# Two transformer blocks on one core in split float16: four norms by logarithm, joint probabilities in differential attention, and four edits at the stage borders

## The reference, cut to what matters

```python
# first block
h = h + mixer_block(rms_norm(h, g), ...)  # differential attention (4 heads, two softmaxes) and windowed GQA
h = h + swiglu(rms_norm(h, g), ...)
attn = softmax(s1) - lam * softmax(s2)    # differential attention, then einsum('bhqk,bkhe->bqhe', attn, v)
# second block, two layers: convolution and MLA; then NSA (compressed, selected and window keys)
x = x + rms_norm_2(m, norm_mix_post); x = x + rms_norm_2(sq_relu_mlp(h, w1, w2), norm_mlp_post)
y = xf * lax.rsqrt(jnp.mean(xf * xf, axis=-1, keepdims=True) + EPS)   # every rms_norm
blk = z[:, idx] + pe[:, None, :]          # NSA: compress(), pe is the bias row
```

## Time and profile before

| | |
|---|---|
| median of 3 runs | 2088.15 us (2085.74 to 2088.97) |
| the profiled execution's own time | 2086.16 us |
| its span in the trace | 2084.4 us |
| PE busy | 2008.0 us, 96% |
| DVE busy | 1183.9 us, 57% |
| ACT busy | 819.6 us, 39% |
| POOL busy | 33.5 us, 2% |
| mean granted TensorE clock | 0.992 of full speed |

### The profile page before, as it was taken

How to read it: one execution, slowest core, us unless ns; L and a number is a source line. 1 busy time by engine, 2 the same in 40 slices (tenths; PEclk the granted TensorE clock), 3 DMA queues, 4 the chain that set the end, 5 groups by cost and what they waited for, 6 DMA issues and landing times. The chain is left out here.

```text
span 2084.4 us, 27136 instructions
## 1 busy us (share of the span) xinstructions
PE 2008.0 (96%) x10509; PEld 945.3 (45%) x10514; DVE 1183.9 (57%) x2158; ACT 819.6 (39%) x1487; POOL 33.5 (2%) x35
## 2 busy tenths in 40 slices
PE   9989999999999999999999999997999999999997
PEld 4444444444444444444444444444544444444443
DVE  5976744546554337776576632358766646864222
ACT  4446733323333232346333322236377743432220
POOL 2000000000000002000000000000000000000000
PEclk9999999999999999999999999999999999999998
DMA  7300223324333322312233333308100031533311
GB/s 216 101 1 1 72 86 106 101 62 141 101 101 111 91 91 78 114 51 72 71 108 113 103 103 99 107 25 255 42 1 1 22 101 41 148 104 105 108 41 41
DMA packets 53191, 179.16 MB, mean 86 GB/s; under 512 B 6096, under 2 KB 9808, under 8 KB 52816
## 3 DMA queue, kind: packets, MB, share of 16 engines
q1 hardware_dynamic: 53072, 177.51, 28.1%
HBM read 174.34 MB, written 2.10 MB: 85 GB/s over the span
## 5 line engine op out<-in xcount | busy, mean ns | idle before, releaser
L1744 DVE SCALAR_TENSOR_TENSOR w_lo<-w_raw,w_hi 128x1024 f16<-128x1024 f32 x317 | 385.5, 1220 | 166.5 <-ACT w_hi L1389 155.6
L1389 ACT ACTIVATE w_hi<-w_raw 128x1024 f16<-128x1024 f32 x317 | 330.8, 1048 | 264.3 <-PE pS L944 258.7
L942 PE MATMUL pS<-xx,w_hi 128*128 128x512 f16 x928 | 351.7, 379 | 2.3 <-DVE xx L1759 1.4
L944 PE MATMUL pS<-xx,w_lo 128*128 128x512 f16 x928 | 351.7, 379 | 0.0
L943 PE MATMUL pS<-xx,w_hi 128*128 128x512 f16 x928 | 351.6, 379 | 0.0
L942 PE MATMUL pS<-arena,w_hi 128*128 128x512 f16 x918 | 347.9, 379 | 2.1 <-DVE arena L1759 1.5
L943 PE MATMUL pS<-arena,w_hi 128*128 128x512 f16 x918 | 347.9, 379 | 0.0
L944 PE MATMUL pS<-arena,w_lo 128*128 128x512 f16 x918 | 347.9, 379 | 0.0
L1398 ACT ACTIVATE arena<-src 128x512 f16<-128x512 f32 x106 | 68.5, 647 | 323.2 <-DVE src L2391 164.0
L1805 DVE TENSOR_TENSOR tmp<-pS,rs 128x512 f32<-128x512 f32 x98 | 67.5, 689 | 137.9 <-PE pS L944 137.9
L942 PEld LDWEIGHTS pS<-arena,w_hi 128*128 128x128 f16 x918 | 89.9, 98 | 111.9 <-DVE arena L1759 1.9
(11 more groups left out here) (331 smaller groups left out, 2643.2 us busy)
## 6 DMA issues: line engine op xcount, KB each, us to landing
w_raw<-in_w SPq DMA_DIRECT2D x317, 512.0 KB, 3.6
X<-in_x SPq DMA_DIRECT2D x8, 264.0 KB, 7.4
arena<-in_c SPq DMA_DIRECT2D x2, 1024.0 KB, 7.6
out_t<-X SPq DMA_DIRECT2D x8, 256.0 KB, 2.0
arena<-in_h SPq DMA_DIRECT2D x4, 256.0 KB, 13.1
arena<-in_h SPq DMA_DIRECT2D x2, 512.0 KB, 10.1
arena<-in_c SPq DMA_DIRECT2D x2, 256.0 KB, 2.9
arena<-arena SPq DMA_DIRECT2D x4, 128.0 KB, 2.6
```

Of the source, the lines that this page charges most:

```text
L942: pe.matmul(ps, wh, ah, start=f, stop=False)
L944: mm = pe.matmul(ps, wl, ah, start=False, stop=l)
L1389: act.activation(w_hi[:, u % WR, :], w_raw[:, u % RAW, :], ACT.Copy, scale=WS).then_inc(hi_split, 1)
L1744: dve.scalar_tensor_tensor(out=w_lo[:, u % WR, :], in0=w_raw[:, u % RAW, :], scalar=WS, in1=w_hi[:, u % WR, :], op0=ALU.mult, op1=ALU.subt ...
```

## The change

- **Norms.** `xb`, `cq`, `p1` and `p3` (`LOGS`) get one 128x512 product of `ones` and `acc` where the four one-column products stood, and ACT's Ln and Exp from it. The mean, POOL's power, the diagonals and the second product go. The factor 1/64 that `rs` held is now a scalar in DVE's evictions, which become `scalar_tensor_tensor`. With the five of `DIRECT`, nine norms go by logarithm.
- **Joint probabilities.** The units of the differential heads are numbered with their halves in turn. DVE forms p1 + nlam * p2 (`combine`, 128x512 float32) after the second exponent of each pair, PE does one product for both, the values times `nlam` go. The `mix` run has eight places for exponents, its products lie three units behind, and a head starts when the rows of both halves are there.
- **Last additions.** DVE scales, POOL adds tiles 0 to 4, DVE adds 5 to 7; SP stores in the order 0, 1, 2, 5, 3, 6, 4, 7.
- **First weight unit.** ACT and DVE split it in two halves of 512 columns; PE starts on the first.
- **Gates.** The four `gt` tiles lie in bank 3, evicted after the last. The first `vv` tile is done whole before the attention.
- **Bias row and z rows.** The bias row is laid out before the norm `mb`; the `z` rows are made with the low part one behind the eviction; POOL fills `kc1` and `kc2`, and `vcz` is filled before `q2`.

```diff
+                elif s.name == "gt":
+                    b = 3
...
+                self.before.append(self.before[s.o0] if s.name == "gt" and j else last.get(b, -1))
...
+LOGS = ("xb", "cq", "p1", "p3")
...
-        if group[0].paired:
-            b = len(group) // 2
-            order = [(group[x + h * b], i) for x in range(b) for i in range(len(group[0].keys)) for h in range(2)]
-            order += [(group[-1], len(group[0].keys))] * group[-1].extra
-            self.values += [[u + x, u + x + 1] for x in range(0, 6 * b, 2)]
-            self.values += [[u + 6 * b]] * group[-1].extra
-        else:
-            order = [(t, i) for t in group for i in range(t.n_units)]
-            self.values += [[u + x] for x in range(len(order))]
+        b, keys = len(group) // 2, len(group[0].keys)
+        order = [(group[x + h * b], i) for x in range(b) for i in range(keys) for h in range(2)]
+        pairs = [[u + x, u + x + 1] for x in range(0, len(order), 2)]
+        order += [(group[-1], keys)] * group[-1].extra
...
+        def exps(u):
+
+            if u < RUNS["mla"].u0 and u % 8 >= 4:
+                return more[:, u % 8 - 4, :]
+            return tmp[:, u % 4, :]
+
+        def ring(u):
+
+            return 8 if u < RUNS["mla"].u0 else 4
...
-            norm_power("xb")
-            pool.wait_ge(rstd_ready, NORM["xb"] + 1)
+            pool.wait_ge(wide_ready, LOGS.index("xb") + 1)
...
-            norm_power("cq")
-            norm_power("p1")
+            pool.wait_ge(mm_done, PL.out_ms[S["dn0"].o0 + KD - 1])
+            fill(kc1, 0.0)
+            for g in range(4):
+                fill(kc2[head_rows(g % 2), g, :], 0.0)
+            assert filled[0] == ZERO_CMP
             norm_power("p2")
-            norm_power("p3")
+            for n in range(SHARED):
+                pool.wait_ge(scaled, n + 1)
+                a = tmp[:, n, :] if n < 4 else src[:, n - 4, :]
+                pool.tensor_tensor(X[:, n, 0:T], X[:, n, 0:T], a, ALU.add).then_inc(added, 1)
...
+                if name in LOGS:
+                    pe.matmul(pT[:, 1, :], ones[:, :], acc[:, 0:T], start=True, stop=True).then_inc(sum_wide, 1)
+                    return
...
-                    pe.matmul(o, extra_values(t), tmp[:, us[0] % 4, :], start=False, stop=True,
-                              skip_group_check=t.paired).then_inc(unit_av, 1)
+                    pe.matmul(o, extra_values(t), exps(us[0]), start=False, stop=True,
+                              skip_group_check=not t.joint).then_inc(unit_av, 1)
+                    return
+                if t.joint:
+                    (kb, _, _, _), = t.keys[i]
+                    pe.wait_ge(combined, JOINT[us[0]] + 1)
+                    pe.matmul(o, values(t, kb), exps(us[0]), start=i == 0, stop=False).then_inc(unit_av, 2)
-                        rows = head_rows(t.half) if t.paired else slice(0, P)
-                        new = t.b == 0 and i == 0 and n_ == 0 and (t.paired or t.first)
-                        mm = pe.matmul(o[rows, q0:q0 + n], values(t, kb), tmp[:, u % 4, c0:c0 + n], start=new, stop=False,
-                                       skip_group_check=t.paired)
+                        rows = head_rows(t.half)
+                        new = t.b == 0 and i == 0 and n_ == 0
+                        mm = pe.matmul(o[rows, q0:q0 + n], values(t, kb), exps(u)[:, c0:c0 + n], start=new, stop=False,
+                                       skip_group_check=True)
...
+                if x < 12:
+                    tile_N(S["vv"], full, 1 + x // 4, x % 4 * 2, x % 4 * 2 + 2)
...
-                        pe.wait_ge(lse_rows, t.lse + 1 + t.paired)
-                    elif t is not None and not t.paired:
-                        pe.wait_ge(lse_rows, t.lse + 1)
+                        pe.wait_ge(lse_rows, t.lse + 2)
...
-                        while now and left[0][-1] <= now[0].u[now[1]] - 2:
+                        while now and left[0][-1] <= now[0].u[now[1]] - (3 if now[0].kind.name in ("diff", "win") else 2):
...
-            tile_N(S["vv"], full, 0, 0, 2)
+            tile_N(S["vv"], full, 0, 0, KD)
...
+                    if u == 0:
+                        act.activation(w_hi[:, 0, 0:UW // 2], w_raw[:, 0, 0:UW // 2], ACT.Copy, scale=WS).then_inc(half_hi, 1)
+                        act.activation(w_hi[:, 0, UW // 2:UW], w_raw[:, 0, UW // 2:UW], ACT.Copy, scale=WS).then_inc(hi_split, 1)
...
+                if name in LOGS:
+                    n = LOGS.index(name) + 1
+                    act.wait_ge(sum_wide, n)
+                    act.activation(rs[:, 0:T], pT[:, 1, :], ACT.Ln, bias=eps[:, :], scale=1.0 / WIDTH[name]).then_inc(wide_log, 1)
+                    act.wait_ge(wide_log, n)
+                    act.activation(rs[:, 0:T], rs[:, 0:T], ACT.Exp, scale=-0.5).then_inc(wide_ready, 1)
+                    return
...
+                    a = 0
+                    if u == 0:
+                        a = UW // 2
+                        dve.wait_ge(half_hi, 1)
+                        dve.scalar_tensor_tensor(out=w_lo[:, 0, 0:a], in0=w_raw[:, 0, 0:a], scalar=WS, in1=w_hi[:, 0, 0:a],
+                                                 op0=ALU.mult, op1=ALU.subtract).then_inc(half_lo, 1)
...
-                dve.tensor_tensor(dst, ps, r[:, 0:T], ALU.mult).then_inc(evicted, 1)
+                if rs_unit[0] == 1.0:
+                    dve.tensor_tensor(dst, ps, r[:, 0:T], ALU.mult).then_inc(evicted, 1)
+                else:
+                    dve.scalar_tensor_tensor(out=dst, in0=ps, scalar=rs_unit[0], in1=r[:, 0:T], op0=ALU.mult,
+                                             op1=ALU.mult).then_inc(evicted, 1)
...
-                evict_N(S["va"], t, vd[:, 0, t, :], T, rn[:, t:t + 1])
-                moved(S["va"], t)
-                link(dve.tensor_scalar(vd[:, 1, t, :], vd[:, 0, t, :], nlam[:, :], None, ALU.mult))
+                evict_N(S["va"], t, vd[:, t, :], T, rn[:, t:t + 1])
...
+            def combine(us):
+
+                dve.wait_ge(key_exped, us[1] + 1)
+                a, b = (exps(u) for u in us)
+                dve.scalar_tensor_tensor(out=a, in0=b, scalar=nlam[:, :], in1=a, op0=ALU.mult, op1=ALU.add).then_inc(combined, 1)
...
+                        if now and joint and joint[0][1] < now[0].u[now[1]]:
+                            combine(joint.pop(0))
...
+                if g_in is None:
+                    places = [tmp[:, n, :] for n in range(4)] + [src[:, n, :] for n in range(2)] + [tmp[:, n, :] for n in range(2)]
+                    for n in range(KD):
+                        if n == KD - 1:
+                            moved(s, n)
+                        if n >= 6:
+                            dve.wait_ge(added, n - 5)
+                        ins = dve.scalar_tensor_tensor(out=places[n], in0=m_view(m, n), scalar=pcol(g_post, n), in1=rs[:, 0:T],
+                                                       op0=ALU.mult, op1=ALU.mult)
+                        if n < SHARED:
+                            ins.then_inc(scaled, 1)
+                            continue
+                        link(ins)
+                        sync()
+                        dve.tensor_tensor(X[:, n, 0:T], X[:, n, 0:T], places[n], ALU.add).then_inc(computed, 1)
...
+            dve.wait_ge(rhs_ready, last_lo[0])
+            link(dve.memset(src[:, 1, :], 0.0))
+            sync()
+            places = src[:, 1, :].rearrange("p (r n) -> p r n", r=16)
+            for c in range(2):
+                ins = dve.tensor_copy(places[:, :, 30 * c:30 * c + 2], pcol("pe", c * CL, CL).rearrange("p (s r) -> p r s", s=2))
+                if c == 0:
+                    link(ins)
+            ins.then_inc(bias_laid, 1)
+            sync()
+            dve.wait_ge(bias_laid, 1)
+            lo(PL.r["pe"], z[1][:, 2, :], src[:, 1, :], z[0][:, 2, :])
...
-            link(dve.memset(tmp[:, 3, :], 0.0))
-            sync()
-            places = tmp[:, 3, :].rearrange("p (r n) -> p r n", r=16)
-            for c in range(2):
-                link(dve.tensor_copy(places[:, :, 30 * c:30 * c + 2], pcol("pe", c * CL, CL).rearrange("p (s r) -> p r s", s=2)))
-            sync()
-            for j in range(4):
-                evict(S["kvc"], j, src[:, j % 2, :])
-                lo(PL.r["z"] + j, z_row(1, j), by_place(src[:, j % 2, :]), z_row(0, j))
-            lo(PL.r["pe"], z[1][:, 2, :], tmp[:, 3, :], z[0][:, 2, :])
-            link(dve.memset(kc1, 0.0))
-            for g in range(4):
-                link(dve.memset(kc2[head_rows(g % 2), g, :], 0.0))
-            link(dve.memset(vcz, 0.0))
+            for j in range(5):
+                if j < 4:
+                    dve.wait_ge(rhs_ready, last_lo[0])
+                    evict(S["kvc"], j, src[:, j % 2, :])
+                if j:
+                    moved(S["kvc"], j - 1)
+                    lo(PL.r["z"] + j - 1, z_row(1, j - 1), by_place(src[:, (j - 1) % 2, :]), z_row(0, j - 1))
...
```

(17 more changed lines are left out.)

78 lines of the change are left out of this document (53 added, 25 removed).

## The result

The changed kernel takes 2066.45 us in the median of 4 runs (2064.7 to 2067.57); the kernel before, run beside it, 2087.07 (2085.74 to 2088.97). The ratio is 0.990, with a 95% interval of 0.9883 to 0.9917, so 1% faster. The forecast was 2062, within 2051 to 2072. The profiled executions have spans of 2084.4 and 2065.1: 19.3 us less, where the sum of the prediction was 26.1.

The account below looks back on a forecast made before the run. The prediction took PE to bound the kernel, busy 2008.0 of 2084.4 us. Its savings 1.1 + 0.5 + 7 + 5.8 + 7 + 3.7 + 1 = 26.1 took the median from 2088.15 to 2062, range 2051 to 2072.

Parts of the forecast that it names:

- Start, `value_a`: Kernel start: halved split of the first weight unit saves 1.1 us; start of mix: four fewer DVE instructions save 0.5.
- Differential heads: Heads in mix: one product for both halves cuts a head from 17.17 to about 15.6 us, saving 7 in all.
- Rival 1: Differential heads: PE stays the bound, heads at 13.7 us, all 13.8 saved, total 2055; chance 0.14.
- rival 2: Differential heads: DVE absorbs the whole saving, heads stay at 17 us, total 2069; chance 0.12.
- the 12.9 for DVE's list: Differential heads: DVE's assumed time per head before combinations, 12.9 us; 2.7 for four combinations brings it to 15.6.
- the bound changes side: Differential heads: DVE at 15.6 us per head against PE at 13.7 becomes the bound and sets the period.
- Norms: Four norms: 5.8 us saved, from xb 2.6, cq 1.6, p1 and p3 0.8 each.
- Bias row, rows, fills: NSA opening: 7.8 us leaves DVE's chain; PE saves 7, a 3.9 wait whole and 3.1 of the w_lo waits' 7.9.
- Gates: NSA gates: a whole vv tile fills PE's 4.2 us wait for DVE's diag; 3.7 saved.
- rival 5: In mix, short PE waits drop the granted clock to the 1.2 GHz level; slower, 2093 us or more; chance 0.015.
- End: Last additions shared by DVE and POOL: 1 us saved, between ends of 3.8 saved and 2.3 longer.
- Rival 3: Kernel end: DVE and POOL lock each other out, 3.4 us worse than the term, total 2065.5; chance 0.28.

Follow-up runs that it names:

- gates_undone: The changed kernel with gate tiles in a bank each and only a quarter of the first vv tile ahead of the attention, as before: 2067.77 us, ratio 0.9908.
- tail_dve: The changed kernel with the last additions all on DVE again (SHARED = 0), none on POOL: 2064.13 us, ratio 0.9884.
- after_again: The changed kernel run once more with no edit: 2066.7 us, ratio 0.9897.
- before: The kernel without the change, run beside the changed one: 2087.07 us in the median.
- z_serial: The changed kernel with DVE making the z rows one after the other again, bias row and fills as changed: 2071.35 us in one run.

## Why the prediction held, and where it did not

**Start, `value_a`.** 1.4 for 1.1 looks better than it is: the split gave 0.96, and 0.43 is a transfer that landed earlier. `value_a` gave 0.66 for 0.5.

**Differential heads.** The period was forecast at 15.6 and is 15.7 to 15.9, and the stage gained 7.6 (7 + 0.5 forecast). Rival 1 (13.7) and rival 2 (17) are out. That the sum fits is partly luck: the parts (first head and start, two heads, last head) are off by 1.5, -0.5 and -1.2 and cancel, and the 12.9 for DVE's list in the 15.6 was taken and not worked out. The reason was half right too. PE's list did fall to 13.6, as "PE would fall to 17.17 - 4 x 0.86 = 13.7" has it, and DVE is the fullest engine. The step that doesn't hold is "the bound changes side", by which the longer of the two lists sets the period. With 2 us taken off DVE the period falls by only 0.5 to 0.8, to 14.9 to 15.4; the rest is pauses of PE, mostly for ACT, that neither list contains. In the changed kernel's second head such pauses are 2.1 of the 15.7: 0.7 and 0.2 ahead of products that wait for ACT's exponents of the row scores, 0.5 for a combination, 0.45 for ACT's squares. And the sentence that three units of distance "let `combine` be late by one unit without a wait", told in passing, is what the gain hangs on: with two, the period is 16.8 to 18.3 and nothing is left.

**Norms.** 6.4 for 5.8, and undoing them costs the same 6.4 in the traces.

**Bias row, rows, fills.** 7.7 for 7, with the parts 4.25, 1.8 and 1.6 (forecast before the overlap: 4.5, 1.8, 1.5). DVE's list moved as a whole: the `w_lo` for which PE waits behind 108 products of `ck1` starts 19.5 after rs of p2 (at 1404.99) and started 27.1 after it before (at 1427.07), and PE follows. Of the 7.7, 5.0 are gained ahead of `ck1`'s first product: the 3.9, and 0.92 that PE no longer waits ahead of its last 48 products of the stage before (`ks`, `kw`), which I hadn't counted. The 2.7 behind it are near the 3.1 that I took from the waits for `w_lo`. These waits went only from 7.9 to 7.3 in sum, because PE gets to them sooner: the first 108 products of `ck1` take 4.8 us instead of 6.4, at a granted clock of 1.00 instead of 0.73. PE then waits for the same DVE instruction, so this gave nothing.

**Gates.** This step failed: 3.7 forecast, nothing that can be told from the scatter measured. It is the sentence "three pieces of `vv` that covered later score steps are moved forward, and a bare step costs under a microsecond more". The cost isn't in the steps but behind them: the row scores run into the logarithm's chain on DVE and ACT sooner, and PE waits 2.7 for it where it had products before. The wait was moved, from 79 us after rs of p2 (`gates_undone`) to 109, and became two thirds as long; it was not removed. Where the 1.5 between the two waits went isn't seen.

**NSA layer as a whole.** 5.3 for 10.7. The opening gave 0.7 more, the gates 3.7 less, so 2.4 are still missing: from q2 to the last square of mc the first trace takes 291.4, the one before 289.0. I had priced the granted clock for `mix` (rival 5, where it stayed at 1.00) and not here. In the row-score stretch it is 0.67 against 0.89 before, and 0.83 against 1.00 ahead of the output product, where 8 products or 1.7 us are lost. An estimate from the same code in `tail_dve` and `after_again`: 10.1 us more at the lower level go with 2.96 us more of time behind the start of q2, 0.29 for each, so the 8.5 us that the first trace has above the one before cost about 2.5. That fits the 2.4. Whether the edits cause some of the drops, or only the places where PE's pauses happened to fall, stays open.

**End.** Rival 3 came true, with 0.28: -1.35 for +1. The price of POOL's addition was right (1.26 for 1.2). The Trainium skill's rule ("SBUF — State Buffer", section "Who interferes with whom"), that a DVE instruction with two inputs in SBUF and a GpSimd one that reads SBUF exclude each other, agrees with the stretched rows of both engines here (1.75 for 0.75 and 1.70 for 1.26). If nothing at all overlapped the end would take 14.4, and the trace has 12.5, so part of each instruction does overlap. From my two ends I chose the middle, which no mechanism stood behind; the only row with both engines at work, the 5.63, spoke for the bad end.

**The sum.** 26.1 was forecast, 19.3 is the difference of the traces, 20.6 that of the medians. The 6.8 between forecast and traces are gates 3.7, end 2.35 and the rest of NSA 2.4, less 1.7 from the terms that came out larger (opening 0.7, norms 0.6, start 0.3, `mix` 0.1). So the time lies in the range because the misses of the NSA layer and the end together, 7.75, are smaller than the 10 that the range left, and not because each term held.

## What to carry to other kernels

When products are taken off a full engine and paid for on another, look first at the distance between producer and consumer, and then at the sum of work: here one number turned a gain of 7.5 us to zero. The longer of two lists is a floor for the period and not its length; here 2.1 us of pauses lay above PE's list of 13.6. A wait that is filled with work taken from later must be followed to where that work was; if it covered a chain there, the wait only moves. Work is not shared between DVE and GpSimd by their durations alone: first look at what one costs while the other runs.

## What the hardware showed unexpectedly

- POOL's addition of 128x512 float32 takes 1.26 us alone and 1.70 to 1.71 beside DVE; DVE's scaling 0.75 alone and 1.74 to 1.75 when it begins beside a POOL addition, DVE's addition 0.69 and 1.63. Together they were slower than DVE alone, 12.5 against 11.2.
- The same stretch of 10 us with PE busy 7.72 and the same two pauses ran at a granted clock of 1.00 in three traces (`before`, `gates_undone`, `z_serial`) and of 0.83 in the other eleven. The pauses in a stretch don't determine by themselves whether the clock falls, and identical code in the NSA layer took 320.75 to 323.76 us, which bounds what one profile can say of a stage.
- Where PE waits for its inputs anyway, as in the NSA opening, the clock doesn't show in the time: q2 began 31.0 to 31.06 us after rs of p2 in all eleven traces with that opening, though the lower level lay at different instructions (from 22.5 us after rs in the first trace, from 20.6 to 24.0 and again from 27.5 in `after_again`).
